# The dense value phase of a PEER layer: larger gate runs, a staged first group, other places for the row sums and the normalisation

## Chip, cores and metric

One core of a Trainium2 chip runs the whole layer. The metric is the time of one execution in microseconds (us); the median of the runs of a kernel is compared.

## The reference, cut to what matters

The layer has a mixer, a cross-attention and a PEER sublayer, 1024 tokens of width 1024, all in float32. Only the end of the PEER sublayer is touched by the change:

```python
def peer_ffn(h, w_pq, sub_keys, expert_u, expert_v):
    ...
    def block(args):
        x_blk, idx_blk, g_blk = args
        u = expert_u[idx_blk]
        a = g_blk * jax.nn.gelu(jnp.einsum('tkd,td->tk', u, x_blk), approximate=False)
        return jnp.einsum('tk,tkd->td', a, expert_v[idx_blk])
...
        ff = peer_ffn(h, w_pq[l], sub_keys[l], expert_u[l], expert_v[l])
        h = layer_norm(DN_ALPHA * h + ff, ln3_g[l], ln3_b[l])
```

There are 16384 experts, and every token picks 128 of them.

## The kernel before

`expert_stages` treats the two halves of the tokens in two ways at once. Rows 0 to 511 (four row tiles of 128 tokens, held in `xg`) are done by gathers: for each token its 128 rows of `expert_u` and of `expert_v` come in by indirect DMA. Rows 512 to 1023 are done densely: all 16384 activations are computed (`act_d`), a gate array `gate_d` holds each token's weight for each expert or zero, and the last stage, called the v phase here, multiplies activations by gates and runs one large matrix product with `expert_v`.

**Dense side.** The v phase walks over 128 expert tiles e of 128 experts, in 32 groups q of four (`GE`). For an expert tile the SP queue loads the activations (`a_raw`, 256 KB) and the rows of `expert_v` (`v_raw`, 512 KB) into two buffers each, and the gates of two expert tiles at a time (`load_gates`, 512 KB). DVE multiplies activations by gates (`multiply`, L1950), ACT rounds values and activations to their high parts (L1926, L1928), and DVE forms the low parts (`low_parts`, L1955 and L1957). PE then does, for each of four token tiles t, 24 matmuls of the group into `ps` (L106 to L108), and DVE adds the result to the accumulator `acc` (`add`, L1964). DVE's step for expert tile 4q+x contains the add of token tile x of group q-1, so DVE's step goes at the pace of PE's tiles. PE starts a group once the low parts of all its four expert tiles are there.

**Gathered side.** It shares the time of the v phase. GpSimd (POOL) issues gathers of 128 rows (512 KB each) in one fixed order, `gathers`, into a ring of 8 slots; gather n waits until gather n-8 has been used. A u gather is used by one `dot` on DVE (L1409), four v gathers by one `values` set on PE (16 narrow matmuls, L1425). `share` spreads both over the steps. Of the work left to the v phase, 96 dots belong to the first 16 groups, 6 in a group, and 64 sets are spread over all 32 groups, two in a group, behind its token tiles t=1 and t=3. Half of the sets belong to row tile 2, the other half, which need the last dots, to row tile 3.

**End.** Behind the last group, `add_residual(dve, 3)` closes the gathered rows, the residual rows of the dense half are loaded and added (L1994), and all eight row tiles are normalised: statistics and gain on DVE (`RowNorm`, L183 to L211), root and scaling on ACT, bias on POOL (L217), store by SP.

## Time and profile before

| | |
|---|---|
| median of 3 runs | 3789.56 us (3776.56 to 3790.67) |
| profiled execution: own time | 3780.85 us |
| profiled execution: span, mean granted clock | 3778.9 us, 0.912 |
| busy: PE, DVE, POOL, ACT | 83%, 56%, 38%, 32% |
| v phase in the span | from 2725.3 us to the end, 1053.6 us |

The span is from the first to the last instruction; the own time holds some 2 us more. Busy shares are averages over stages with different limits, so the v phase is read by itself, in stretches that begin where PE starts a group. Group q below is PE's group q.

### The profile page before, as it was taken

What the parts mean: (1) busy time and instruction counts of PE and PEld (TensorE: products, weight loads), DVE (VectorE), ACT (ScalarE), POOL (GpSimd) and SP (SyncE); (2) the same over time, 40 slices, a digit from 0 to 9 for tenths busy, and PEclk for the clock granted to TensorE, in tenths of its full rate; (3) what the DMA queues carried; (4) which work ended last, traced back from release to release, by engine and by line L of the source; (5) the groups of instructions that cost most, each with busy time, mean ns of one, the idle gap of its engine ahead of it and who ended that gap; (6) DMA issues with size and microseconds to landing.
All of it is one profiled execution on the core that took longest, in us unless ns stands there. A gap on an engine that the chain in (4) does not pass through costs nothing. (4 is left out here: it accounts for less than half of the span.)

```text
span 3778.9 us, 42789 instructions
## 1 busy us (share of the span) xinstructions
PE 3131.4 (83%) x16184; PEld 2426.7 (64%) x16184; DVE 2127.0 (56%) x4487; ACT 1201.8 (32%) x1931; POOL 1446.9 (38%) x1116
## 2 busy tenths in 40 slices
PE   4995978888799899999999985565378787899994
PEld 3874766777688788887777763444255565566663
DVE  4134764115422568988777765455365665555556
ACT  3113541314211244443333325666421211222221
POOL 2101011401200055557776774565445444422222
PEclk9996799899899899999999997777688998999997
DMA  4333022323222379989999996888899999988883
GB/s 151 108 98 114 1 79 87 122 75 101 94 68 67 128 298 353 335 338 397 410 410 408 411 406 242 319 296 320 302 328 343 329 341 328 330 310 308 309 311 143
DMA packets 368046, 937.45 MB, mean 248 GB/s; under 512 B 31441, under 2 KB 130265, under 8 KB 366817
## 3 DMA queue, kind: packets, MB, share of 16 engines
q0 software_dynamic: 147456, 536.94, 37.9%
q1 hardware_dynamic: 220384, 397.77, 29.9%
q8 instruction: 130, 2.13, 0.2%
q14 instruction: 76, 0.61, 0.0%
HBM read 827.60 MB, written 106.98 MB: 247 GB/s over the span
## 5 line engine op out<-in xcount | busy, mean ns | idle before, releaser
L1400 POOL DMA_INDIRECT ex_ring<-in_expert_v,ex_idxT_sb x455 | 504.4, 1109 | 604.0 <-PE ex_ps_v L1425 452.6
L1400 POOL DMA_INDIRECT ex_ring<-in_expert_u,ex_idx_sb x345 | 456.0, 1322 | 430.9 <-DVE ex_hg L1409 241.8
L1409 DVE CUSTOM_DVE_ANT_0 ex_ring<-ex_ring,ex_xg 128x1024 f32<-128x1024 f32 x345 | 413.1, 1219 | 254.7 <-DMA ex_ring<-in_expert_u,ex_idx_sb 253.8
L106 PE MATMUL eo_ps<-eo_v_hi_sb,aT_late_hi 128*128 128x512 f32 x1024 | 409.5, 400 | 41.4 <-DVE aT_late_lo L1957 41.4
L1425 PE MATMUL ex_ps_v<-ex_ring,ex_w_sb 128*32 128x512 f32 x1820 | 284.2, 716 | 170.7 <-DMA ex_ring<-in_expert_v,ex_idxT_sb 167.7
L106 PE MATMUL ex_ps_h<-aT_late_hi,ex_uT_hi_sb 128*128 128x512 f32 x1024 | 413.0, 403 | 1.9 <-ACT ex_uT_lo_sb L1541 1.1
L107 PE MATMUL eo_ps<-eo_v_lo_sb,aT_late_hi 128*128 128x512 f32 x1024 | 402.1, 393 | 0.0
L108 PE MATMUL ex_ps_h<-aT_late_hi,ex_uT_lo_sb 128*128 128x512 f32 x1024 | 401.8, 392 | 0.0
L107 PE MATMUL ex_ps_h<-aT_late_lo,ex_uT_hi_sb 128*128 128x512 f32 x1024 | 400.3, 391 | 0.0
L108 PE MATMUL eo_ps<-eo_v_hi_sb,aT_late_lo 128*128 128x512 f32 x1024 | 400.0, 391 | 0.0
L1964 DVE TENSOR_TENSOR eo_acc<-eo_acc,eo_ps 128x1024 f32<-128x1024 f32 x124 | 151.4, 1221 | 417.5 <-PE eo_ps L108 417.5
L1926 ACT ACTIVATE eo_v_hi_sb<-eo_v_raw 128x1024 fp32r<-128x1024 f32 x128 | 135.8, 1061 | 574.1 <-DMA eo_v_raw<-in_expert_v 574.1
L106 PEld LDWEIGHTS eo_ps<-eo_v_hi_sb,aT_late_hi 128*128 128x128 f32 x1024 | 193.7, 189 | 145.4 <-DVE aT_late_lo L1957 55.3
L1854 PE MATMUL ex_ps_x<-ex_hw,ex_hot 128*128 128x128 f32 x1024 | 172.8, 338 | 115.2 <-ACT ex_gate L1810 109.6
L1400 POOL DMA_INDIRECT ex_ring_more<-in_expert_u,ex_idx_sb x167 | 213.9, 1281 | 137.7 <-DVE ex_hg L1409 75.1
L1854 PEld LDWEIGHTS ex_ps_x<-ex_hw,ex_hot 128*128 128x128 f32 x1024 | 159.4, 245 | 152.7 <-issue 146.8
L1541 ACT ACTIVATE ex_uT_lo_sb<-ex_ps_t 128x1024 fp32r<-128x1024 f32 x128 | 131.7, 1029 | 379.8 <-PE ex_ps_t L1719 379.8
L1425 PEld LDWEIGHTS ex_ps_v<-ex_ring,ex_w_sb 128*32 128x32 f32 x1820 | 59.3, 124 | 296.7 <-issue 296.1
L106 PEld LDWEIGHTS ex_ps_h<-aT_late_hi,ex_uT_hi_sb 128*128 128x128 f32 x1024 | 193.0, 188 | 77.8 <-issue 30.0
L1409 DVE CUSTOM_DVE_ANT_0 ex_ring_more<-ex_ring_more,ex_xg 128x1024 f32<-128x1024 f32 x167 | 199.4, 1221 | 53.1 <-DMA ex_ring_more<-in_expert_u,ex_idx_sb 50.6
L108 PEld LDWEIGHTS eo_ps<-eo_v_hi_sb,aT_late_lo 128*128 128x128 f32 x1024 | 193.7, 189 | 41.8
L108 PEld LDWEIGHTS ex_ps_h<-aT_late_hi,ex_uT_lo_sb 128*128 128x128 f32 x1024 | 193.2, 189 | 42.6
(322 smaller groups left out, 6535.1 us busy)
## 6 DMA issues: line engine op xcount, KB each, us to landing
ex_u_raw<-in_expert_u SPq DMA_DIRECT2D x128, 512.0 KB, 8.2
eo_v_raw<-in_expert_v SPq DMA_DIRECT2D x128, 512.0 KB, 5.5
act_d<-ex_act SPq DMA_DIRECT2D x128, 256.0 KB, 6.0
gate_d<-ex_gate SPq DMA_DIRECT2D x8, 4096.0 KB, 15.9
eo_g_raw<-gate_d SPq DMA_DIRECT2D x64, 512.0 KB, 6.5
eo_a_raw<-act_d SPq DMA_DIRECT2D x128, 256.0 KB, 4.4
h_d<-n_row SPq DMA_DIRECT2D x24, 512.0 KB, 2.6
pin_raw<-in_w_in SPq DMA_DIRECT2D x20, 512.0 KB, 3.9
```

Source lines behind the costliest of these rows:

```text
L106: pe.matmul(ps, l_hi, r_hi, start=first, stop=False)
L107: pe.matmul(ps, l_hi, r_lo, start=False, stop=False)
L108: return pe.matmul(ps, l_lo, r_hi, start=False, stop=last)
L1400: pool.indirect_dma_start(rows(n), None, table, bass.IndirectOffsetOnAxis(at, 0)).then_inc(ring_in[slot[n]], 16)
L1409: dve.tensor_tensor_reduce(out=u, in0=u, in1=xg[:, j, :], scale=1.0, scalar=0.0, op0=ALU.mult, op1=ALU.add, accum_out=hg[:, j, k:k + 1]).t ...
L1425: last = pe.matmul(ps_v[32 * q:32 * q + 32, col], spreads[:, q, 31 * i + 31:31 * i + 63], rows(at[q])[:, col], start=i == 0, stop=i == 31)
L1541: act.activation(uT_lo[:, e % 2, :, :], ps_t[e % 2][:].rearrange("p (k t) -> p k t", t=P), ACT.Copy).then_inc(uT_lo_done, 1)
L1854: last = pe.matmul(ps_x[b % 2][:, x * P:(x + 1) * P], hot1[:, s, 4 * y + x, :], hw[:, s, 4 * y + x, :], start=True, stop=True)
L1926: act.activation(v_hi[:, b, x, :], v_raw(e), ACT.Copy).then_inc(v_hi_done, 1)
L1964: dve.tensor_tensor(acc[:, t, :], acc[:, t, :], ps[t % 2][:], ALU.add).then_inc(added[t % 2], 1)
```

## The change

Seven edits, all in the v phase and in the lists that feed it.

1. `load_gates` loads the gates of four expert tiles (1 MB, in two DMAs), so that each run in memory is 1 KB where it was 512 B. The second buffer for them is the part of `xg` that held row tiles 0 and 1.
2. These two row tiles, finished before, are written to `kept` (the dead DRAM buffer `h0_d`) at the start of the phase and come back into ring slots 0 and 1 at expert tile 114.
3. The four expert tiles of group 0 are loaded without waiting for each other, values into `acc`, activations into `v_sb`.
4. The residual rows of the dense half are loaded into `acc` during group 0's matmuls, and the first `add` scales and adds them; the four L1994 instructions at the end go.
5. The 96 dots are spread over the first 60 steps in place of 64. No set of values stands in groups 0, 16 and 28 to 31; 32 sets stand in groups 1 to 15 and 32 in groups 17 to 27.
6. Row tiles 0 to 3 are normalised inside groups 29 and 30 of DVE's and ACT's programs (`LN_TILES`); the order of a step is multiply, add, low parts, then the pieces of the normalisation.
7. Only row tiles 4 to 7 are normalised behind the last group, each as soon as its last add is done.

```diff
+            LAST_VALS, LN_TILES = 112, GROUPS - 3
+
+            def dots_b(e):
+                return share(DOTS_B, ETILES // 2 - 4, e) if e < ETILES // 2 - 4 else 0
+
+            def vals_b(e):
+                half = ETILES // 2
+                if GE <= e < half:
+                    return share(P // 4, half - GE, e - GE)
+                if half + GE <= e < LAST_VALS:
+                    return share(P // 4, LAST_VALS - half - GE, e - half - GE)
+                return 0
...
                     def a_raw(e):
-                        return a_sb[:, e % 2, :]
+                        return v_sb[:, e // 2, e % 2 * DN:(e % 2 + 1) * DN] if e < GE else a_sb[:, e % 2, :]
 
                     def v_raw(e):
-                        return v_sb[:, e % 2, :]
+                        return acc[:, e, :] if e < GE else v_sb[:, e % 2, :]
+
+                    def g_raw(r):
+                        flat = g_sb[:] if r % 2 == 0 else xg[:, 0:2, :].rearrange("p j d -> p (j d)")
+                        return flat.rearrange("p (n e t) -> p n e t", e=GE, t=GBLK)
...
                             def load_gates(r):
                                 if r >= 2:
-                                    sp.wait_ge(prod, 2 * (r - 1))
-                                sp.dma_start(g_raw[:, r % 2, :, :, :], gate_d[:, :, 2 * r:2 * r + 2, :].rearrange("n p e t -> p n e t")).then_inc(g_in[r % 2], 16)
...
+                                    sp.wait_ge(prod, GE * (r - 1))
+                                for h in range(2):
+                                    n = slice(h * NBLK // 2, (h + 1) * NBLK // 2)
+                                    sp.dma_start(g_raw(r)[:, n, :, :], gate_d[n, :, GE * r:GE * (r + 1), :].rearrange("n p e t -> p n e t")).then_inc(g_in[r % 2], 16)
+
+                            for e in range(GE):
+                                sp.dma_start(v_raw(e), v_rows[e, :, :]).then_inc(first_in[e], 16)
+                                sp.dma_start(a_raw(e), act_d[e, :, :]).then_inc(first_in[e], 16)
+                                if e == 0:
+                                    load_gates(0)
+                            for j in range(2):
+                                sp.wait_ge(sum_g, j + 1)
+                                sp.dma_start(kept[j * P:(j + 1) * P, :], xg[:, j, :]).then_inc(kept_out[j], 16)
...
+                                if e == GE:
+                                    for j in range(2):
+                                        sp.wait_ge(kept_out[j], 16)
+                                    load_gates(1)
+                                if e < 2 * GE:
+                                    t = e - GE
+                                    sp.wait_ge(v_lo_done, t + 1)
+                                    sp.dma_start(acc[:, t, :], resid[(GT + t) * P:(GT + t + 1) * P, :]).then_inc(row_in[t], 16)
+                                if e % GE == 2 and e // GE + 1 < GROUPS:
+                                    load_gates(e // GE + 1)
...
                                 if q == 0:
-                                    dve.tensor_copy(acc[:, t, :], ps[t % 2][:]).then_inc(added[t % 2], 1)
+                                    dve.wait_ge(row_in[t], 16)
+                                    dve.scalar_tensor_tensor(acc[:, t, :], acc[:, t, :], ALPHA, ps[t % 2][:], ALU.mult, ALU.add).then_inc(added[t % 2], 1)
...
+                                    if LN_TILES <= q < LN_TILES + GT // 2:
+                                        j = 2 * (q - LN_TILES) + x // 2
+                                        if x % 2 == 0:
...
+                                            ln.statistics(dve, j, whole_row(j))
+                                        else:
+                                            ln.scale(dve, j)
+                                        if x % 2 == 0 and j >= 1:
+                                            ln.times_gain(dve, j - 1, whole_row(j - 1))
...
-                                    for _ in range(share(VALS_B // 4, ETILES, q * GE + t)):
+                                    for _ in range(vals_b(q * GE + t)):
                                         values(pe, done)
                                         done += 4
```

Three places show how the instructions stand. The first is SP's queue at the start of the v phase, before the change; `act_d` are the activations and `gate_d` the gates.

```order
L1887 DMA eo_g_raw<-gate_d 128x8x128 x2
L1894 DMA eo_a_raw<-act_d 128x512
L1897 DMA eo_v_raw<-in_expert_v 128x1024
L1894 DMA eo_a_raw<-act_d 128x512
L1897 DMA eo_v_raw<-in_expert_v 128x1024
```

And the same place in the changed kernel:

```order
L1919 DMA eo_acc<-in_expert_v 128x1024
L1920 DMA eo_v_raw<-act_d 128x512
L1916 DMA eo_g_raw<-gate_d 128x4x256 x2
L1919 DMA eo_acc<-in_expert_v 128x1024
L1920 DMA eo_v_raw<-act_d 128x512
```

Two more such pairs follow, then two writes of kept rows (`h_d<-ex_xg`), and the regular loads begin. The queue of group 0 also takes in the gates of group 1 and four residual rows.

The second place is POOL's list of gathers at the start of the v phase, before:

```order
L1400 DMA ex_ring<-in_expert_u,ex_idx_sb 128x1024
L1400 DMA ex_ring<-in_expert_v,ex_idxT_sb 128x1024 x4
L1400 DMA ex_ring<-in_expert_u,ex_idx_sb 128x1024 x3
L1400 DMA ex_ring<-in_expert_v,ex_idxT_sb 128x1024 x4
L1400 DMA ex_ring<-in_expert_u,ex_idx_sb 128x1024 x3
```

And after:

```order
L1415 DMA ex_ring<-in_expert_u,ex_idx_sb 128x1024 x8
L1415 DMA ex_ring<-in_expert_v,ex_idxT_sb 128x1024 x4
L1415 DMA ex_ring<-in_expert_u,ex_idx_sb 128x1024 x3
L1415 DMA ex_ring<-in_expert_v,ex_idxT_sb 128x1024 x4
L1415 DMA ex_ring<-in_expert_u,ex_idx_sb 128x1024 x3
L1415 DMA ex_ring<-in_expert_v,ex_idxT_sb 128x1024 x4
L1415 DMA ex_ring<-in_expert_u,ex_idx_sb 128x1024 x3
L1415 DMA ex_ring<-in_expert_v,ex_idxT_sb 128x1024 x4
L1415 DMA ex_ring<-in_expert_u,ex_idx_sb 128x1024 x4
```

Seven more u gathers stand ahead of the first four v gathers, and further on the pieces of three u are now and then four, or one.

The third place is DVE in group 29, expert tiles 118 and 119. Before, a step there was these four rows over and over:

```order
L1950 TENSOR_TENSOR eo_a_raw<-eo_a_raw,eo_g_raw 128x512
L1964 TENSOR_TENSOR eo_acc<-eo_acc,eo_ps 128x1024
L1955 TENSOR_TENSOR eo_v_lo_sb<-eo_v_raw,eo_v_hi_sb 128x1024
L1957 TENSOR_TENSOR aT_late_lo<-eo_a_raw,aT_late_hi 128x512
L1950 TENSOR_TENSOR eo_a_raw<-eo_a_raw,eo_g_raw 128x512
```

After, the statistics of row tile 1 and the gain of row tile 0 (both in the ring) stand between two steps:

```order
L1996 TENSOR_TENSOR eo_a_raw<-eo_a_raw,ex_xg 128x512
L2011 TENSOR_TENSOR eo_acc<-eo_acc,eo_ps 128x1024
L2001 TENSOR_TENSOR eo_v_lo_sb<-eo_v_raw,eo_v_hi_sb 128x1024
L2003 TENSOR_TENSOR aT_late_lo<-eo_a_raw,aT_late_hi 128x512
L183 BN_STATS eo_ln_stats<-ex_ring 128x6 x2
L184 BN_AGGR eo_ln_mv<-eo_ln_stats 128x2
L185 TENSOR_SCALAR eo_ln_var_sb<-eo_ln_mv 128x1
L211 TENSOR_TENSOR ex_ring<-ex_ring 128x1024
L1996 TENSOR_TENSOR eo_a_raw<-eo_a_raw,ex_xg 128x512
L2011 TENSOR_TENSOR eo_acc<-eo_acc,eo_ps 128x1024
L2001 TENSOR_TENSOR eo_v_lo_sb<-eo_v_raw,eo_v_hi_sb 128x1024
L2003 TENSOR_TENSOR aT_late_lo<-eo_a_raw,aT_late_hi 128x512
```

## Rows read from the trace of the kernel before

**Rows 1.** Stretches of the v phase: start, group 0, 1 to 14, 15, 16 to 31, end.

```profile
core 0: us, PE busy (x) PEld busy (x) DVE busy (x) ACT busy (x) POOL busy (x), PEclk, DMA share, GB/s
2725.30:2749.40 24.10, 0.45 (x1) 0.18 (x1) 15.73 (x23) 6.53 (x8) 4.89 (x4) 0.50 0.82 285
2749.40:2786.60 37.20, 30.60 (x129) 21.12 (x129) 23.98 (x33) 8.35 (x10) 15.10 (x12) 0.82 0.86 299
2786.60:3268.10 481.50, 390.26 (x1793) 267.83 (x1794) 295.83 (x393) 94.12 (x113) 227.25 (x196) 0.90 0.95 336
3268.10:3295.20 27.10, 25.90 (x129) 18.58 (x130) 13.74 (x16) 4.97 (x6) 8.63 (x9) 1.00 0.90 325
3295.20:3728.30 433.10, 415.15 (x2037) 298.94 (x2041) 218.46 (x246) 101.38 (x121) 118.80 (x124) 1.00 0.83 295
3728.30:3778.90 50.60, 1.80 (x16) 0.29 (x12) 41.65 (x62) 11.54 (x16) 18.75 (x8) 0.57 0.33 125
```

**Rows 2.** Timeline of PE in group 8: its two sets of values.

```profile
3036.46 1.92 PE L1425 MATMUL ex_ps_v<-ex_ring,ex_w_sb 128*32 128x512 f32 x16 [0.17 <-DMA ex_ring<-in_expert_v,ex_idxT_sb]
3055.02 3.64 PE L1425 MATMUL ex_ps_v<-ex_ring,ex_w_sb 128*32 128x512 f32 x16 [5.53 <-DMA ex_ring<-in_expert_v,ex_idxT_sb]
```

**Rows 3.** Timeline of DVE and POOL ahead of the second set.

```profile
3039.21 1.22 DVE L1409 CUSTOM_DVE_ANT_0 ex_ring<-ex_ring,ex_xg 128x1024 f32<-128x1024 f32 x1
3040.71 1.68 POOL L1400 DMA_INDIRECT ex_ring<-in_expert_u,ex_idx_sb  x1 [4.29 <-DVE ex_hg L1409]
3046.42 1.43 POOL L1400 DMA_INDIRECT ex_ring<-in_expert_v,ex_idxT_sb  x1 [0.30 <-issue]
```

**Rows 4.** The gather line, groups 1 to 14: ns min/median/max; who waits; landing.

```profile
L1400 POOL DMA_INDIRECT ex_ring<-in_expert_v,ex_idxT_sb x115: 932/938/1892, 2786.9 to 3264.2; - x115
L1400 POOL DMA_INDIRECT ex_ring<-in_expert_u,ex_idx_sb x81: 933/1142/1683, 2790.6 to 3249.2; - x81
...
  PE ex_ps_v L1425: 91.2, 15
...
DMA to landing us min/median/max: 5.0/6.7/10.9
```

**Rows 5.** DMA in groups 1 to 14: queues, then issues with KB and median landing.

```profile
q0 software_dynamic: 28234, 102.81, 58.2%
q1 hardware_dynamic: 45292, 58.84, 36.2%
...
eo_a_raw<-act_d SPq DMA_DIRECT2D x56, 256.0 KB, 4.7
eo_g_raw<-gate_d SPq DMA_DIRECT2D x28, 512.0 KB, 9.5
```

**Rows 6.** Stretches with much and with little in 512 B runs; columns as Rows 1.

```profile
2000.00:2100.00 100.00, 95.33 (x495) 72.33 (x494) 81.94 (x245) 35.12 (x40) 68.01 (x56) 0.98 1.03 409
2728.00:2731.00 3.00, 0.00 (x0) 0.00 (x0) 0.00 (x0) 0.00 (x0) 0.00 (x0) 0.50 1.15 327
```

**Rows 7.** Timeline of PE in the second half: sets behind t=3, t=1, t=3.

```profile
3428.31 1.92 PE L1425 MATMUL ex_ps_v<-ex_ring,ex_w_sb 128*32 128x512 f32 x16
3442.57 1.92 PE L1425 MATMUL ex_ps_v<-ex_ring,ex_w_sb 128*32 128x512 f32 x16
3455.57 1.92 PE L1425 MATMUL ex_ps_v<-ex_ring,ex_w_sb 128*32 128x512 f32 x16
```

**Rows 8.** Timeline of PE from group 30 to group 31.

```profile
3700.91 1.92 PE L1425 MATMUL ex_ps_v<-ex_ring,ex_w_sb 128*32 128x512 f32 x16
...
3704.03 0.50 PE L106 MATMUL eo_ps<-eo_v_hi_sb,aT_late_hi 128*128 128x512 f32 x1 [1.20 <-DVE aT_late_lo L1957]
```

**Rows 9.** Timeline of DVE and POOL in the end stretch.

```profile
3730.16 1.22 DVE L1458 SCALAR_TENSOR_TENSOR ex_xg<-ex_xg,ex_ps_v 128x1024 f32<-128x1024 f32 x1 [0.66 <-PE ex_ps_v L1425]
3733.75 1.41 DVE L183 BATCH_NORM_STATS2 eo_ln_stats<-ex_xg 128x6 f32<-128x512 f32 x2
3735.52 1.22 DVE L211 TENSOR_TENSOR ex_xg<-ex_xg,ex_w_sb 128x1024 f32<-128x1024 f32 x1
3744.07 3.27 DVE L1994 SCALAR_TENSOR_TENSOR eo_acc<-eo_v_raw,eo_acc 128x1024 f32<-128x1024 f32 x1
...
3743.91 2.34 POOL L217 TENSOR_TENSOR ex_xg<-ex_xg,ex_w_sb 128x1024 f32<-128x1024 f32 x1 [1.16 <-DVE ex_xg L211]
...
3773.51 2.34 POOL L217 TENSOR_TENSOR eo_acc<-eo_acc,ex_w_sb 128x1024 f32<-128x1024 f32 x1 [1.16 <-DVE eo_acc L211]
```

More of the change, by code:

```diff
@@ L1253, in _, with expert_stages @@
                         scores(HP - 1)
-        def expert_stages(gain, bias, resid, dest):
+        def expert_stages(gain, bias, resid, kept, dest):
             GT = 4
@@ L1317, in expert_stages @@
             END_G = len(gathers)
-            for n in range(GE * (GROUPS + 1)):
-                for _ in range(share(DOTS_B, ETILES // 2, n) if n < ETILES // 2 else 0):
+            for e in range(ETILES + GE):
+                for _ in range(dots_b(e)):
                     gathers.append(("u", nu))
                     nu += 1
-                for _ in range(4 * share(VALS_B // 4, ETILES, n - GE) if n >= GE else 0):
+                for _ in range(4 * vals_b(e - GE)):
                     gathers.append(("v", nv))
@@ L1362, in expert_stages @@
             row_in = [sem(f"eo_row_in{i}") for i in range(DT)]
-            sum_done, stored = sem("eo_sum"), sem("eo_stored")
+            first_in = [sem(f"eo_first_in{i}") for i in range(GE)]
+            kept_out, kept_in = [[sem(f"eo_kept_{w}{i}") for i in range(2)] for w in ("out", "in")]
+            stored = sem("eo_stored")
             with ExitStack() as whole:
@@ L1862, in expert_stages @@
                     sb, pb = local(stage)
[L1863 removed]
+                    ln = RowNorm("eo_ln", sb, gain, bias, rows=(ring[:, 2, :], ring[:, 3, :]))
                     acc = sb("eo_acc", [P, DT, D])
[L1865 removed]
+                    a_sb, v_sb, g_sb = sb("eo_a_raw", [P, 2, DN]), sb("eo_v_raw", [P, 2, D]), sb("eo_g_raw", [P, 2 * D])
                     a_hi, a_lo = [w[:].rearrange("p (b x) t -> p b x t", b=2) for w in (late_hi, late_lo)]
@@ L1907, in _ @@
+                                if e < 2 * GE:
[4 more added lines that the diff above has]
+                                    load_gates(e // GE + 1)
+                                if e == LAST_VALS + 2:
                                     sp.wait_ge(val_done, GT * P // 4)
+                                    for j in range(2):
+                                        sp.dma_start(whole_row(j), kept[j * P:(j + 1) * P, :]).then_inc(kept_in[j], 16)
@@ L1968, in _ @@
                             spread_weights(dve, 2)
-                            for q in range(GROUPS + 1):
+                            for q in range(GROUPS):
                                 if q == VAL_TILE:
```

90 lines of the change are left out of this document (43 added, 47 removed).

## Prediction

> **What bounds the kernel now.** I read first the stretches of the v phase, because nothing before 2725 us changes [rows 1]. There are three regimes.
>
> In groups 1 to 14 a group takes 481.5 / 14 = 34.4 us, while in group 15, which has the same matmuls and the same two sets but no dots beside it, it takes 27.1 us. The 7 us between them are PE waiting. The timeline of PE says for what: the set behind t=1 starts at once, the one behind t=3 waits 5.5 us for its gathers and then takes 3.64 us where 1.92 is usual [rows 2]; in the 14 groups such waits are 91.2 us, 15 times [rows 4]. Following one back: the tile t=1 ends about 3036.3, DVE does its add and low parts and then the dot at 3039.21, which frees the slot for the u gather at 3040.71, four v gathers must follow it in POOL's order, the last is issued at 3046.42, and the set starts at 3055.02 [rows 2, 3]. So this stretch is set by the ring. In numbers: 115 + 81 = 196 gathers, 14 a group, 2.46 us a gather, so that with 8 slots a slot turns round in 19.7 us, of which the landing (median) is only 6.7 [rows 4]. The rest is order and waiting for PE's and DVE's steps. The DMA engines are nearly always busy too, 0.95 [rows 1], but at 336 GB/s, where the same core moves 409 at a share of 1.03 earlier on [rows 6]. So they are loaded, and not quite the limit.
>
> In groups 16 to 31 the 433.1 us are PE's own [rows 1]. A set and two tiles take 13.00 us and, over a group boundary, 14.26 [rows 7]. At the boundary PE ends its last tile at about 3700.9, DVE has still to add, and to make the low parts of the last expert tile, and PE starts again at 3704.03: 3.1 us, of which a set behind t=3 hides 1.9 [rows 8]. So a tile is about 5.5 us, a set not at t=3 costs 2.0, a boundary 3.1 whether a set lies in it or not: 16 x 22.0 + 15 x 3.1 + 16 x 2.0 = 430.5, against 433.1 measured.
>
> In the end stretch, 50.6 us, DVE is busy for 41.7 and PE for 1.8 [rows 1].
>
> **The change, part by part.**
>
> *Start.* Now 24.1 us, in which DVE works 15.7 [rows 1]; the staged loads remove only what DVE waits between the four expert tiles, since four dots and the same splitting stay. The first multiply still has 1.75 MB ahead of it or with it. Gain 0 to 4, I take 2.
>
> *Group 0* has no sets any more. From 37.2 go the two sets, 1.9 and 3.5, and a wait of some 6.5; its boundary is bare again, +3.1. The new instruction that waits is the first add of a token tile, for its residual row; behind it in DVE stand the low parts of group 1. The residual row of t=3 is queued behind 1 MB of gates and the loads of expert tiles 6 and 7, and 1 MB of kept rows has gone out before. I give this 1 us; at worst it is 8. New 29.3, so 8 gained.
>
> *Groups 1 to 13.* Dots go from 6 to 6.4 a group, v gathers from 8 to 8.53: 14.93 gathers where there were 14. If the ring keeps its 2.46 us a gather, a group takes 36.7, and 13 groups 477.1 in place of 447.2: 30 lost. The other bound is that the transfers set the pace. The two queues take 58.2% and 36.2% of 34.4 us [rows 5], which is 20.0 for 14 gathers (1.43 each) and 12.5 for the loads. The added 0.93 gathers are +1.3. The gates: in the stretch that is mostly 512 B runs the core moves 327 GB/s, and 409 in one with few of them [rows 6], so a group's 1.05 MB takes 3.2 us and, if 1 KB runs brought it all the way, 2.6. By the share (1.15 against 1.03) it is a little more. I take 0.8 saved, between 0 and 1.1. Then a group is (32.5 + 1.3 - 0.8) / 32.5 x 34.4 = 34.9, and 13 groups lose 7. I take the ring's end, because of the 19.7 us only 6.7 are landing, so lighter transfers shorten little of it.
>
> The Trainium skill's page "DMA: Bandwidth & Descriptors", section Specifications, gives 512 B as the smallest transfer that reaches line rate; by it 1 KB runs would save nothing, and the transfers' end would be 35.8 a group. The trace disagrees in part: 327 against 409 GB/s. By either, the ring's 36.7 stays.
>
> *Groups 14 and 15.* The dots are over, and each is PE's own: four tiles, boundary, and two sets not at t=3, 22.0 + 3.1 + 4.0 = 29.1. Together 58.2 where 34.4 + 27.1 = 61.5 stood: 3 gained.
>
> First half in all: -2 - 8 + 30 - 3 = +17.
>
> *Groups 16 to 31.* The same 32 sets now stand in 11 groups, and in only 8 of these one stands at t=3. The boundaries behind groups 16 to 19 and 28 to 30 are bare. By the formula, 352 + 46.5 + 24 x 2.0 = 446.5, and with the 2.6 that the formula lacks 449.1: +16. The sets of three tiles in a row ask for their last gathers 12.7 us after a slot comes free, and four issues (about 1.24 apart) with a landing of 6.7 need 10.4 to 12; I add 4 for late ones.
>
> The normalisation in groups 29 and 30 costs DVE time in steps that are now only 5.5 us. A step is 3.5; statistics add 1.8 and the gain 1.1 [rows 9]. Then POOL adds the bias, 2.34, and while it runs, a DVE instruction with two operands in SBUF waits: L1994 takes 3.27 beside POOL's L217, and the same operation with one operand in PSUM takes 1.22 [rows 9]. The multiply and the low parts have two such operands. Walking through the steps, the low parts of the last expert tile are 2.0 late in group 29 and 2.8 in group 30. PE waits both: +5. Second half: 16 + 4 + 5 = +25.
>
> *End.* PE's last tile, then DVE: add 1.1, statistics 1.8, gain of the tile before 1.2, scale 0.3, then ACT 1.3, gain about 2 with POOL in the way, POOL 2.34, and from its end to the end of the span 3.05 [rows 1, 9]: 13.2 with the small gaps. It was 50.6 behind the same tile. Gain 37.4.
>
> *Hidden.* The return of the kept rows and the gain and bias loads come when DMA has no gathers left. The first adds cost as much as the copies they replace.
>
> **Sum.** +17 + 25 - 37.4 = +4.6. Against the profiled execution's own 3780.85 that is 3785.5. The median of the runs is 8.7 above that execution and the lowest 4.3 below; the mean of all four is 3784.4. I forecast 3786, that is, no change. Half a per cent, 19 us, is about what can be told from nothing.
>
> **The rivals.**
>
> *Transfers set the first half (faster).* For it speak the DMA share of 0.95 [rows 1], and that the gates' landing is 9.5 us among gathers, against 4.7 for the activations [rows 5]: fewer, larger packets could let all else land sooner. Against it the 336 GB/s. Groups 1 to 13 then lose 7 in place of 30: 3785.5 - 23 = 3762.5. If also the late sets of the second half vanish, 3758.
>
> *The loads fall behind in groups 17 to 27 (slower).* A group there has 11.6 gathers, where groups 16 to 31 have 8: 11.6 x 1.43 + 12.5 - 0.8 = 28.3 us of transfers in 29.5 us of PE, a share of 0.96, as in the first half. Activations of expert tile 4q+3 are issued one step after the 1 MB of gates and are needed about two steps after them, some 15 us, with up to 4 more until the add waits for PE. The gates' 512 KB took 9.5 among gathers; 1 MB in as many packets as 512 KB had, but longer ones, takes 10 to 14, and the activations 5 more: 15 to 19. It decides from 19 on. If it is 2 us late in 11 groups, +22: 3807; 3 us, 3818.
>
> The same page, section Queues, rings and completion order, says each DMA engine takes a packet from each queue in turn. By that rule the gates' small packets wait for a gather's large one each time, as the 9.5 us suggest, and halving their number should shorten this wait. No row shows 1 KB runs.
>
> *The end gives nothing back.* It would need that DVE or POOL were not what holds the end stretch; DVE's 41.7 of 50.6 exclude it.
>
> **Chances.** Forecast, within 0.5%: 0.45, own range 3770 to 3803. Transfers set the pace: 0.30. Loads fall behind: 0.25. From these faster 0.30, same 0.45, slower 0.25. The range reaches to the first rival's 3758 and a little below, and over the second's milder form: 3756 to 3811, about 0.2 left out.
>
> **What the profile after would show.** The end stretch behind PE's last eo_ps matmul is 11 to 16 us. Groups 1 to 13 take 36 to 37.5 us with gather waits of 5 to 9 us before a set in most groups; if they take under 35, the transfers' theory holds. Groups 28 to 30 have no L1425 line (now L1440), and a wait of 3 to 6 us on the low parts ahead of each group. In groups 17 to 27 DVE should not wait for DMA at the multiply; if it does, for tens of us in total, the second rival holds. I am wrong by more than the range if group 0 stalls on the kept rows, or if the granted clock falls in groups that now wait longer.

## The result, and the profile after

The changed kernel takes 3840.58 us (median of 4 runs, 3834.19 to 3843.32), the kernel before beside it 3785.32 (4 runs). The ratio is 1.0146, 95% interval 1.0130 to 1.0163: slower by 55 us, where 3786 was forecast.

The stretches of the v phase after the change, cut where PE starts group 0, 1, 14 and 16 and behind its last matmul (us; busy time and count of PE, PEld, DVE, ACT, POOL; clock; DMA share; GB/s). They answer to [rows 1], where the second cut behind group 0 is at group 15 in place of 14:

```profile
2725.30:2745.00 19.70, 0.00 (x0) 0.00 (x0) 14.06 (x21) 7.47 (x9) 5.41 (x4) 0.50 1.02 381
2745.00:2776.50 31.50, 24.27 (x97) 19.57 (x97) 22.41 (x31) 5.60 (x7) 8.78 (x7) 0.88 0.96 358
2776.50:3266.30 489.80, 378.33 (x1681) 257.15 (x1681) 279.56 (x375) 87.27 (x105) 221.50 (x191) 0.89 0.88 316
3266.30:3326.70 60.40, 56.15 (x273) 38.84 (x274) 31.21 (x38) 13.63 (x17) 19.36 (x19) 0.97 0.80 287
3326.70:3824.90 498.20, 434.49 (x2049) 310.25 (x2049) 244.12 (x295) 107.07 (x134) 133.95 (x130) 0.95 0.73 264
3824.90:3838.10 13.20, 0.00 (x0) 0.00 (x0) 6.25 (x9) 1.83 (x3) 5.92 (x3) 0.63 0.29 119
```

The end stretch fell from 50.6 to 13.2 us, as worked out. The forecast for the first half was +17; start, group 0, groups 1 to 13 and groups 14 and 15 came to -4.4, -5.6, +42.7 and -1.2, in all +31.5 (before, groups 1 to 13 took 447.1 and groups 14 and 15 61.7). The second half was to cost +25 and cost +65 (498.2 against 433.1). In both the DMA engines are less busy than before (0.88 and 0.73, before 0.95 and 0.83), and the clock of PE is lower (0.95 against 1.00 in the second half). So on average the DMA engines had less to do, not more; PE waited in more places, and slowed down behind the waits. In groups 1 to 13 its waits for gathers are about the same before (first row) and after (second row); new are the waits for the low parts at the start of a group (third row, with the 7.2 ahead of group 1), of which there were none:

```profile
PE ex_ps_v L1425 <- DMA ex_ring<-in_expert_v,ex_idxT_sb: 84.4, 14, 7.7
PE ex_ps_v L1440 <- DMA ex_ring<-in_expert_v,ex_idxT_sb: 89.1, 15, 7.9
PE eo_ps L106 <- DVE aT_late_lo L2003: 26.4, 9, 7.2
```

The table of waits for groups 15 to 31 (who, for what: us, times, longest) names one that was not there before, DVE's for activations, and one that has grown: PE waits 66.7 us for low parts where it had 18.0. The longest wait of either kind belongs to group 28 and is explained under group 27.

```profile
PE eo_ps L106 <- DVE aT_late_lo L2003: 66.7, 16, 14.5
DVE eo_a_raw L1996 <- DMA eo_a_raw<-act_d: 45.3, 10, 16.6
```

**Groups 18 to 23** take 203.9 us in all, 34.0 each. Their three sets stand behind t=0, 1 and 2 in groups 18 and 19, behind t=0, 1 and 3 in 20 to 22, behind t=0, 2 and 3 in 23, and the timeline of group 18 (SP's issues, then DVE and ACT, then PE) shows what happens:

```profile
3392.30 1.63 SPq L1916 DMA_DIRECT2D eo_g_raw<-gate_d  x2
3399.02 0.33 SPq L1929 DMA_DIRECT2D eo_a_raw<-act_d  x1
...
3405.87 0.69 DVE L2003 TENSOR_TENSOR aT_late_lo<-eo_a_raw,aT_late_hi 128x512 fp32r<-128x512 f32 x1
3411.73 0.69 DVE L1996 TENSOR_TENSOR eo_a_raw<-eo_a_raw,ex_xg 128x512 f32<-128x512 f32 x1 [5.17 <-DMA eo_a_raw<-act_d]
...
3414.28 1.06 ACT L1967 ACTIVATE eo_v_hi_sb<-eo_v_raw 128x1024 fp32r<-128x1024 f32 x1 [14.01 <-DMA eo_v_raw<-in_expert_v]
...
3415.37 1.22 DVE L2001 TENSOR_TENSOR eo_v_lo_sb<-eo_v_raw,eo_v_hi_sb 128x1024 fp32r<-128x1024 f32 x1 [1.82 <-ACT eo_v_hi_sb L1967]
...
3417.25 0.79 PE L106 MATMUL eo_ps<-eo_v_hi_sb,aT_late_hi 128*128 128x512 f32 x1 [6.06 <-DVE aT_late_lo L2003]
```

The gates of the next group, 1 MB, are issued at 3392.30, the activations of the fourth expert tile at 3399.02, its values right behind them; POOL issues twelve gathers between 3390.60 and 3409.55. The multiply is ready at 3406.6 and starts at 3411.73, 19.4 us after the gates' issue and 12.7 after its own load's. The values land later still, at 3414.3, and DVE waits another 1.82 us until ACT has split them. PE then waits 6.06 at the boundary, where a bare boundary is 3.05. So it is the values, queued behind the late activations, that end last here; in groups 20 to 22 DVE waits 0.50 to 0.55 us for them behind the late multiply. Later on, in groups 24 to 26, with three sets a group as well, but spread to t=0, 2 and 3 or 1, 2 and 3, PE has no such wait. The first row below is groups 18 to 22, the second 24 to 26 (columns as above); the late loads fall where the DMA share is 0.82, not where it is 0.97.

```profile
3381.20:3553.20 172.00, 148.15 (x720) 100.17 (x720) 71.59 (x81) 33.88 (x41) 58.98 (x60) 0.95 0.82 304
3585.10:3673.20 88.10, 84.51 (x433) 57.13 (x433) 42.92 (x49) 19.41 (x24) 34.75 (x37) 1.00 0.97 355
```

**Group 27** took 42.6 us. PE's timeline has its longest wait at the start of group 28, and the waits of SP's own queue show why: SP stood for 17.4 us, until the last set of values, ahead of the loads of the two kept rows (L1948).

```profile
3715.82 0.79 PE L106 MATMUL eo_ps<-eo_v_hi_sb,aT_late_hi 128*128 128x512 f32 x1 [14.48 <-DVE aT_late_lo L2003]
```

```profile
SPq L1948 <- PE ex_ps_v L1440: 17.4, 1, 17.4
```

**Groups 1 to 13** are not even: with sets behind t=1 and 3 (groups 1 to 3, 9 to 11) they average 35.5, in groups 5 to 7, 12 and 13, where they stand behind t=0 and 2, 39.9. (Group 4 has t=1 and 2, group 8 three sets.)

### The profile page after: what moved, and what is told of

It is laid out like the page before. It is cut to its first block and busy times, and to the rows that moved or that the text cites. A ratio compares the mean times of both kernels' runs of the same rounds, so it can differ in the third digit from the quotient of the medians.

```text
span 3838.1 us, 42758 instructions
## 1 busy us (share of the span) xinstructions
PE 3156.1 (82%) x16184; PEld 2442.2 (64%) x16184; DVE 2116.9 (55%) x4483; ACT 1198.1 (31%) x1931; POOL 1446.2 (38%) x1116
## 5 line engine op out<-in xcount | busy, mean ns | idle before, releaser
L106 PE MATMUL eo_ps<-eo_v_hi_sb,aT_late_hi 128*128 128x512 f32 x1024 | 424.0, 414 | 117.8 <-DVE aT_late_lo L2003 117.8
L107 PE MATMUL eo_ps<-eo_v_lo_sb,aT_late_hi 128*128 128x512 f32 x1024 | 413.0, 403 | 0.0
L108 PE MATMUL eo_ps<-eo_v_hi_sb,aT_late_lo 128*128 128x512 f32 x1024 | 410.0, 400 | 0.0
L2011 DVE TENSOR_TENSOR eo_acc<-eo_acc,eo_ps 128x1024 f32<-128x1024 f32 x124 | 151.3, 1220 | 438.4 <-PE eo_ps L108 438.3
L106 PEld LDWEIGHTS ex_ps_h<-aT_late_hi,ex_uT_hi_sb 128*128 128x128 f32 x1024 | 192.8, 188 | 77.5 <-issue 29.8
L107 PEld LDWEIGHTS eo_ps<-eo_v_lo_sb,aT_late_hi 128*128 128x128 f32 x1024 | 201.1, 196 | 40.2
```

Of the source, the lines that this page charges most:

```text
L106: pe.matmul(ps, l_hi, r_hi, start=first, stop=False)
L107: pe.matmul(ps, l_hi, r_lo, start=False, stop=False)
L108: return pe.matmul(ps, l_lo, r_hi, start=False, stop=last)
L2011: dve.tensor_tensor(acc[:, t, :], acc[:, t, :], ps[t % 2][:], ALU.add).then_inc(added[t % 2], 1)
```

## The experiments

The work ahead of the v phase is the same in all kernels, but takes from 2742.8 to 2776.4 us by the profiled executions. The medians come from several chips, on which the kernel before takes 3779.7 to 3804.6, so rows are compared by their ratios and not by their medians. Beside the ratio of whole times (each against the kernel before on the same chip) this table gives the profiled stretch from PE's first matmul of the v phase to the end of the span, and parts of it; these are of one execution each.

| kernel | median us | ratio (95%) | v stretch | groups 1-13 | 17-27 |
|---|---|---|---|---|---|
| before | 3785.3 | | 1029.5 | 447.1 | 299.8 |
| after | 3840.6 | 1.0146 (1.0130-1.0163) | 1093.1 | 489.8 | 364.0 |
| late wait moved | 3837.0 | 1.0101 (1.0074-1.0129) | 1074.3 | 482.6 | 353.7 |
| + gate halves | 3806.9 | 1.0038 (1.0012-1.0064) | 1044.0 | 469.6 | 335.3 |
| + sets at t=1,2,3 | 3813.6 | 1.0045 (1.0027-1.0064) | 1043.3 | 484.0 | 320.8 |
| + odd sets, first half | 3796.6 | 0.9992 (0.9973-1.0011) | 1032.9 | 445.0 | 351.4 |
| all four | 3732.6 | 0.9873 (0.9857-0.9890) | 997.9 | 439.5 | 322.4 |
| + one row tile a group | 3724.0 | 0.9855 (0.9836-0.9874) | 975.7 | 423.2 | 323.5 |
| + double steps even | 3723.1 | 0.9788 (0.9766-0.9809) | 944.5 | 384.3 | 320.8 |
| same, sets from group 0 | 3708.2 | 0.9745 (0.9723-0.9768) | 943.6 | 388.1 | 322.4 |

"+" in the fourth to sixth row is added to the moved wait alone; "all four" are the moved wait and these three, and below it each is added to the row above.

### The late wait

```diff
-                                if e == LAST_VALS + 2:
+                                if e == LAST_VALS + 5:
```

> The changed kernel with one move: SP's wait for the last set of values, and the four loads behind it, stand behind expert tile 117 in place of 114. Theory A (SP's wait holds the loads of expert tile 115, which PE needs for group 28): group 27 falls from 42.6 us to 29 to 30, the wait of 14.5 us ahead of group 28 to 3, and the run is about 13 us faster than the changed kernel, 3827. Rival (group 28 waits because 2 MB of returning rows and gains stand ahead of its loads in the queue, wherever the wait is): the wait moves to group 28 or 29 and the time changes by under 4 us.

Group 27 went from 42.64 to 29.39 us, and PE starts group 28 after an ordinary wait:

```profile
3716.34 0.50 PE L106 MATMUL eo_ps<-eo_v_hi_sb,aT_late_hi 128*128 128x512 f32 x1 [1.20 <-DVE aT_late_lo L2003]
```

So the wait for the last set at expert tile 114 cost 13 us: SP reached it while PE was still in group 27, and the loads of tile 115 were queued behind it. The rival, that the returning rows delay group 28 wherever the wait stands, is out. The whole time agrees by its ratio (1.0101 against 1.0146, 17 us), not by its median, since the kernel before takes 3796.8 on this chip. All edits below to the changed kernel are made on top of this one.

### Gates in two steps; other places in the second half

```diff
-                                if e % GE == 2 and e // GE + 1 < GROUPS:
-                                    load_gates(e // GE + 1)
+                                if e % GE in (1, 2) and e // GE + 1 < GROUPS:
+                                    load_gates(e // GE + 1, (e % GE - 1,))
```

> As the kernel with the late wait, and the two halves of a group's 1 MB of gates are issued behind expert tiles 4q+1 and 4q+2 in place of both behind 4q+2. Theory B (in groups 18 to 23 the activations of expert tile 4q+3 land late because 1 MB of gates stands ahead of them): DVE's waits for the activations, 45 us after group 15, fall under 20, groups 18 to 23 go from 204 us towards 180, 15 to 25 us faster than the late wait alone. Rival (the sets behind t=0, 1, 2 call their twelve gathers into the same 20 us, whatever the gates do): under 8 us faster.

```diff
                 if half + GE <= e < LAST_VALS:
-                    return share(P // 4, LAST_VALS - half - GE, e - half - GE)
+                    return 1 if e % GE and e != 69 else 0
```

> As the kernel with the late wait, but the 32 sets of groups 17 to 27 stand behind t=1, 2 and 3 (group 17 has two), as already in groups 26 and 27. Every boundary of these groups is then covered. Theory B' (clumps of gathers at t=0, 1, 2 over the gates make the loads late, and bare boundaries add 3 us): groups 17 to 27 take 29.4 us each, 323 us in place of 350, 20 to 28 us faster. Rival (2.9 sets a group are too many transfers wherever they stand, share 0.96): under 8 us faster.

The first leaves every gather where it was and only issues half of the gates one step earlier: groups 18 to 23 go from 206.9 to 187.2 us (180 was expected; the boundaries behind groups 18 and 19 stay bare). The second leaves the loads and moves the sets away from t=0: groups 18 to 27 take 29.35 each, which is 22.0 + 3.1 + 2 x 2.0 and the 0.2 that the formula lacked. DVE's wait for activations over the second half, in the first and in the second kernel:

```profile
DVE eo_a_raw L1996 <- DMA eo_a_raw<-act_d: 5.2, 6, 1.7
```

```profile
DVE eo_a_raw L1996 <- DMA eo_a_raw<-act_d: 3.8, 4, 1.5
```

It was 27.3 us in the kernel with the late wait alone. Either edit takes nearly all of it away, so it took both, 1 MB of gates in one step and the three sets close together.

### What a bare boundary costs

The kernel before, with its 64 sets behind t=0 and t=2 in place of t=1 and t=3:

```diff
-                for _ in range(4 * share(VALS_B // 4, ETILES, n - GE) if n >= GE else 0):
+                for _ in range(4 * (1 - n % 2) if n >= GE else 0):
...
-                                    for _ in range(share(VALS_B // 4, ETILES, q * GE + t)):
+                                    for _ in range(1 - t % 2):
```

> The kernel before with one change: its 64 sets stand behind t=0 and t=2 of each group in place of t=1 and t=3. Same work, same number of gathers in a group. Theory C (what costs is the boundary that no set, and no wait for one, covers): groups 1 to 14 go from 34.4 us to 38 to 40, groups 16 to 30 from 27.26 to 29.1 to 29.4, so 50 to 75 plus 30 us slower than before: 3865 to 3890. Rival (the place of a set does not matter where gathers set the pace): groups 1 to 14 stay at 34 to 35, only 30 us slower.

It takes 3846.21 us, ratio 1.0152 (1.0122 to 1.0182). In groups 16 to 30 nothing but this place differs: 30.7 us in place of 27.26, so 3.45 for a set that leaves t=3, where the working had 2.0. Of this, 1.85 are idle time (3.05 at a boundary in place of 1.20); the other 1.6 are PE's slower work. Behind each 3.05 us of idle time it starts at the lower clock, and the mean granted clock over 200 us, six and a half such groups, is 0.95 (first row), in the kernel before 1.00 (second).

```profile
3400.00:3600.00 200.00, 181.69 (x845) 129.75 (x845) 92.78 (x104) 43.00 (x52) 50.48 (x52) 0.95 0.76 269
```

```profile
3400.00:3600.00 200.00, 190.43 (x939) 136.06 (x939) 103.19 (x116) 48.14 (x58) 57.90 (x60) 1.00 0.87 308
```

Cut finer, at the boundary at 3427.77: the granted clock is 0.50 (1.2 GHz) for the 3.3 us that begin with PE's start, and 1.00 (2.4 GHz) from there to the next boundary.

```profile
3427.40:3430.70 3.30, 2.93 (x7) 2.38 (x8) 0.92 (x2) 0.63 (x1) 0.00 (x0) 0.50 1.02 382
3430.80:3458.00 27.20, 24.60 (x122) 17.23 (x121) 13.24 (x15) 6.02 (x7) 7.73 (x8) 1.00 0.74 261
```

So the first matmuls behind such a wait are 0.43 us apart from the second on, and 0.23 once the clock is full.

```profile
3427.77 0.80 PE L106 MATMUL eo_ps<-eo_v_hi_sb,aT_late_hi 128*128 128x512 f32 x1 [3.05 <-DVE aT_late_lo L1957]
3428.36 0.63 PE L107 MATMUL eo_ps<-eo_v_lo_sb,aT_late_hi 128*128 128x512 f32 x1
3428.78 0.63 PE L108 MATMUL eo_ps<-eo_v_hi_sb,aT_late_lo 128*128 128x512 f32 x1
```

### The first half: places, rhythm, or loads

```diff
                 if GE <= e < half:
-                    return share(P // 4, half - GE, e - GE)
+                    return e % 2 + (e in (58, 62))
```

> As the kernel with the late wait, but the 32 sets of groups 1 to 15 stand behind t=1 and t=3, with the two extra ones behind t=2 of groups 14 and 15. The number of gathers in a group is as in the changed kernel. Theory C (a group boundary with no set behind t=3 costs its 3.05 us on top of the wait for gathers, and the groups with sets at t=0 and 2 take 39.9 us where those with t=1 and 3 take 35.5): groups 1 to 13 go from 490 us to about 462, 25 to 30 us faster. Rival (the ring sets the pace by its gathers alone, or transfers do): under 8 us faster.

Groups 1 to 13 went from 482.6 to 445.0 us, 34.2 a group. The expectation takes the number of gathers as unchanged, which is not quite so: with the extra sets in groups 14 and 15, two sets a group and 6.4 dots make 14.4, and POOL issues 185 gathers in groups 1 to 13 where it issued 191. At the ring's 2.46 us each, 14.4 gathers ask for 35.4, so this run alone does not decide against the ring; the price of a gather in it, 2.41 us, is near the old one. And in the kernel above, sets behind t=0 and 2 had cost the first half almost nothing (451.2 against 447.1). Two more kernels, profiled in one execution each, split this up; the first is the changed kernel with the old dots (96 over 64 steps), the second the old kernel with sets behind t=0 and 2 and the new dots (96 over 60 steps).

```diff
-                return share(DOTS_B, ETILES // 2 - 4, e) if e < ETILES // 2 - 4 else 0
+                return share(DOTS_B, ETILES // 2, e) if e < ETILES // 2 else 0
```

> The changed kernel with the late wait and with the dots over 64 steps, 3 in 2 steps, as before the change; its sets stay where the change put them. If it is the dots' new rhythm together with sets at t=0 and 2 that costs, groups 5 to 8, 12 and 13 fall from 38 to 42 us to 34 to 36, 20 to 30 us less in the first half. If the loads do it (1 MB of gates at once), they stay at 38 to 42.

```diff
-                                        for _ in range(share(DOTS_B, ETILES // 2, q * GE + x)):
+                                        for _ in range(share(DOTS_B, 60, q * GE + x) if q < 15 else 0):
```

> The kernel before with its sets at t=0 and 2 and the dots over 60 steps, 8 in 5. If the rhythm and the place together suffice, its groups 1 to 13 rise from 34.7 us to 37 to 41. If they need the new loads too, they stay at 34 to 36.

They took 3830.77 and 3909.78 us, groups 1 to 13 471.5 and 500.7. The first fell short of what was expected of the old rhythm: 11 us less in groups 1 to 13, not 20 to 30, and group 14 gave 8 of them back (37.3 us in place of 29.3). The second has none of the new loads and is slow all the same, so these are not needed for it. Its groups go in a pattern of five: groups 4 and 9 take 35, the others 37 to 41. With 1.6 dots a step, the steps with two dots wander, and a set's four v gathers start later when its own step has two. The rows are DVE's dots, POOL's first v gather and PE's set, in the second of these kernels (group 3):

```profile
2893.65 1.22 DVE L1409 CUSTOM_DVE_ANT_0 ex_ring<-ex_ring,ex_xg 128x1024 f32<-128x1024 f32 x1
2894.80 1.22 DVE L1409 CUSTOM_DVE_ANT_0 ex_ring<-ex_ring,ex_xg 128x1024 f32<-128x1024 f32 x1
...
2897.13 0.94 POOL L1400 DMA_INDIRECT ex_ring<-in_expert_v,ex_idxT_sb  x1 [0.30 <-issue]
...
2910.53 3.64 PE L1425 MATMUL ex_ps_v<-ex_ring,ex_w_sb 128*32 128x512 f32 x16 [6.79 <-DMA ex_ring<-in_expert_v,ex_idxT_sb]
```

and in the kernel of the section before, with the old rhythm, where the step has one dot (group 3 too):

```profile
2869.54 1.22 DVE L1409 CUSTOM_DVE_ANT_0 ex_ring<-ex_ring,ex_xg 128x1024 f32<-128x1024 f32 x1
...
2871.04 1.15 POOL L1400 DMA_INDIRECT ex_ring<-in_expert_v,ex_idxT_sb  x1 [7.46 <-DVE ex_hg L1409]
...
2883.92 3.00 PE L1425 MATMUL ex_ps_v<-ex_ring,ex_w_sb 128*32 128x512 f32 x16 [4.29 <-DMA ex_ring<-in_expert_v,ex_idxT_sb]
```

From the first dot to the first v gather it is 3.48 us with two dots and 1.50 with one, since a u gather stands ahead in POOL's order and takes the slot that the first dot frees. To test it, the old kernel with two dots in even steps and one in odd ones (before: one and two), the list of gathers changed with them, with sets at either place:

```diff
-                                        for _ in range(share(DOTS_B, ETILES // 2, q * GE + x)):
+                                        for _ in range(2 - x % 2 if q < GROUPS // 2 else 0):
```

> The kernel before with its sets behind t=0 and t=2 and the dots still 1.5 a step in the first 64 steps, but two in the even steps and one in the odd ones (before: one and two). If what matters is where a step with two dots stands ahead of the gathers of the second set, each of groups 1 to 13 is like the late ones of the kernel with 1.6 dots a step: 37 to 41 us, and PE's first matmul of a group follows a bare boundary of 3.05. If what matters is only that 1.6 dots are more than 1.5, a group stays at 34 to 35 as with sets behind t=0 and 2 and the old rhythm.

> The same dots, two in the even steps and one in the odd ones, but the sets at the old places, t=1 and t=3. If the set at t=3 takes up what the dots' places cost, a group stays at 33 to 35 us. If the dots' places cost by themselves, it is 37 or more as in the other kernel.

One execution each: 3922.75 and 3727.51 us, against 3786.02 for the kernel before beside them. The first came as expected. The second did not: the two answers on record were 33 to 35 us a group, or 37 and more, and it took 29.8. With the sets at their old places the list of gathers is the same as before, only DVE does every third dot one step sooner. So the ring rule falls here: the same 182 gathers take 2.46 us each in one order of dots and 2.12 in the other. All of it together, in us a group (mean of groups 1 to 13, one execution a cell; the left cell of the second row is the changed kernel with its new loads, all others are the old one):

| dots in a set's own step | sets behind t=1, 3 | behind t=0, 2 |
|---|---|---|
| one | 29.8 | 34.7 |
| one or two, wandering | 34.2 | 38.5 |
| two | 34.4 (before) | 38.9 |

Each row and each column has its price: 4.2 to 4.6 us for the double step in a set's own step, 4.3 to 4.9 for the bare boundary. PE's waits in groups 1 to 13 say the same: from the kernel before to the fast corner (the cell of 29.8) its waits for gathers fall from 84.4 to 42.6 us, and from the fast corner to the cell at its right 13 boundary waits of 3.05 come in while the waits for gathers stay (41.2). The rest comes with the granted clock, which is 0.90 before, 0.99 in the fast corner and 0.93 at its right. So the even sets had cost the first half nothing only because they left the double steps as well, and the two cancelled. That the wandering rhythm costs nearly as much as the constant double step is measured and not explained. In the fast corner the DMA engines are busy throughout (groups 0 to 14 of that kernel, all but the last 1.6 us):

```profile
2768.60:3213.10 444.50, 396.44 (x1908) 285.56 (x1912) 312.48 (x419) 98.73 (x120) 224.89 (x206) 0.98 1.02 383
```

That transfers are the limit there is read from this share and not shown by a run.

### 1 KB runs

```diff
...
-                                    n = slice(h * NBLK // 2, (h + 1) * NBLK // 2)
-                                    sp.dma_start(g_raw(r)[:, n, :, :], gate_d[n, :, GE * r:GE * (r + 1), :].rearrange("n p e t -> p n e t")).then_inc(g_in[r % 2], 16)
+                                    sp.dma_start(g_raw(r)[:, :, 2 * h:2 * h + 2, :], gate_d[:, :, GE * r + 2 * h:GE * r + 2 * h + 2, :].rearrange("n p e t -> p n e t")).then_inc(g_in[r % 2][h], 16)
...
```

The gates in 512 B runs again, two expert tiles at a time and at their old places; first with the odd sets of the first half, then in the version with one row tile a group.

> The kernel with the first-half sets at t=1 and 3, with gates again in 512 B runs, two expert tiles a load, at the old places in SP's queue; all else as there. Theory of the ring (a gather costs its turn whatever the loads do): groups 1 to 13 stay at 445 us. Theory of the transfers (1 KB runs and fewer packets are what let 14.9 gathers a group take 34.2 us where 14 took 34.4): 13 x 2 = 20 to 35 us more. In groups 18 to 23 the smaller loads should also remove some of the lateness of the activations, 197 us towards 185.

> The kernel with one row tile normalised a group, with gates in 512 B runs and two expert tiles a load at the old places in SP's queue. Theory of the transfers (1 KB runs save DMA time that PE sees): 10 us or more slower. Theory that the size of the runs does not reach the end time, only how the gates are spread over the steps: within 6 us of that kernel, on either side.

They took 3761.99 us, ratio 0.9958 (0.9942 to 0.9974), and 3740.12, ratio 0.9876 (0.9856 to 0.9896). Groups 1 to 13 took 434.2 and 438.4 us; with 1 KB runs the same sets gave 445.0, 439.5 and 423.2. The last two of these are the same program there, so 16 us is what one execution differs from another, and the runs' length is worth nothing beyond it. The old places also spread the gates over the steps, which is why groups 18 to 23 fall from 203.0 to 190.8 us in the first of the two. The second is 8 us slower by its ratio than its neighbour with 1 KB runs (0.9855), with intervals that overlap: neither of its two expectations, within 6 us or 10 and more. By the Trainium skill, page "DMA: Bandwidth & Descriptors", section Specifications, 512 B is already enough for line rate: these runs agree.

### The normalisation

```diff
-            LAST_VALS, LN_TILES = 112, GROUPS - 3
+            LAST_VALS, LN_TILES = 112, GROUPS + 1
...
+                            for j in range(GT):
...
+                                ln.statistics(dve, j, whole_row(j))
+                                if j >= 1:
+                                    ln.times_gain(dve, j - 1, whole_row(j - 1))
+                                ln.scale(dve, j)
```

> The kernel with the late wait, and all eight row tiles normalised behind the last group (the residual is still added first). Theory D: groups 28 to 30 lose their lag, 84 us become 75 to 76, and the end stretch grows from 13 to 33 to 36 us: in sum about 12 us slower than the late wait alone. It also prices what normalising inside the groups gives: 21 us for 9. Rival (no lag by the normalisation): groups 28 to 30 stay at 84.

With all eight row tiles normalised behind the last group (and the late wait moved) it takes 3844.17 us, 1.0176 (1.0159 to 1.0193). Groups 28 to 30 take 78.6 us in place of 84.0, so the normalisation in them cost 5.4 as the prediction had it (+5; the expectation above has 8 to 9), and the stretch behind the last matmul is 37 us in place of 13.

```diff
-                                    if LN_TILES <= q < LN_TILES + GT // 2:
-                                        j = 2 * (q - LN_TILES) + x // 2
-                                        if x % 2 == 0:
+                                    if q >= LN_TILES:
+                                        j = q - LN_TILES
+                                        if x == 0:
...
-                                        else:
+                                        elif x == 1:
                                             ln.scale(dve, j)
-                                        if x % 2 == 0 and j >= 1:
-                                            ln.times_gain(dve, j - 1, whole_row(j - 1))
+                                        elif x == 2:
+                                            ln.times_gain(dve, j, whole_row(j))
...
```

> As the kernel with all three, but one row tile is normalised in each of groups 29, 30 and 31, its gain two steps behind its statistics, and the fourth behind the last low parts. Theory D (two row tiles a group make DVE late, and PE waits 5.4 and 6.0 us for the low parts ahead of groups 29 and 30 where 3.05 is bare): groups 28 to 30 go from 27.5, 30.3 and 27.6 us to 25 to 26 each, 8 to 10 us faster than all three, and the end stretch stays within 2 us of 13. Rival (the gain and bias collide with DVE's steps in any place): under 3 us.

This is the version with all four edits above, and one row tile normalised in each of groups 29, 30 and 31, in DVE's steps x=0 (statistics), 1 (scale) and 2 (gain), the fourth behind the last low parts. Groups 28 to 30 take 77.6 us in place of 86.2; the waits ahead of groups 29 and 30 are 3.27 and 3.26, near the bare 3.05, where they had been 5.39 and 5.98:

```profile
3629.40 0.50 PE L106 MATMUL eo_ps<-eo_v_hi_sb,aT_late_hi 128*128 128x512 f32 x1 [3.27 <-DVE aT_late_lo L2006]
3654.72 0.58 PE L106 MATMUL eo_ps<-eo_v_hi_sb,aT_late_hi 128*128 128x512 f32 x1 [3.26 <-DVE aT_late_lo L2006]
```

### Put together

> The changed kernel with the late wait, the gate halves apart, the sets of groups 1 to 15 at t=1 and 3, and those of groups 17 to 27 at t=1, 2 and 3. If the causes found (SP's wait 13 us, bare boundaries in the first half 37, clumps and bare boundaries in the second 32, of which the gate halves alone had given 20) lie apart, groups 1 to 13 take about 440 us, 17 to 27 take 321, and from PE's first dense matmul to the end it is 990 to 1000 us, against 1029.5 before: 30 us faster than the kernel before, ratio 0.991 to 0.993. Rival (the waits only move): 1015 or more.

> The kernel with one row tile normalised a group, but dots over 64 steps and sets at t=1 and 3 from group 0 on, just as before the change: 14 gathers a group, 1 KB gates in halves. If the gathers of a group set its pace, groups 1 to 14 take 33 to 34 us each, about 470 in all, where that kernel takes 423 for 1 to 13 and 30.2 for 14, so 15 us slower or more, since group 14 is again among the slow ones and group 0 has its sets back. If gates and staging had helped the first half by themselves, groups 1 to 14 would fall under 32 each.

```diff
             def dots_b(e):
-                return share(DOTS_B, ETILES // 2 - 4, e) if e < ETILES // 2 - 4 else 0
+                return 2 - e % 2 if e < ETILES // 2 else 0
```

> The fastest version so far (odd sets in groups 1 to 15, sets at t=1, 2, 3 in groups 17 to 27, half gates, one row tile normalised a group; 3724 us), with the dots two in even and one in odd steps up to expert tile 63. If the place of the double steps is what the first half waits for, groups 1 to 13 go from 423 us to about 13 x 29.7 = 386 and the time to about 3685. If the effect belongs to the gather list of the old kernel, it stays at 3715 to 3730.

> The same, but with the sets behind t=1 and t=3 from group 0 on as in the kernel before (its form with the old rhythm took 3756 us, groups 0 to 15 550 us). With the new place of the double steps groups 0 to 15 should take some 472 us as in the kernel before with the same dots, and the time be about 3680. Without the effect it stays at 3756.

All four edits gave 3732.64. The first half with dots and sets as in the kernel before gave 3756.13, ratio 0.9925 (0.9908 to 0.9941), groups 1 to 13 451.5: all else in the change, mended, is worth 0.75% by itself. With the double dots in even steps its groups 1 to 13 take 388.1 and the kernel 3708.22 us, ratio 0.9745 (0.9723 to 0.9768), 2.5% faster than before; 3680 had been expected, on a chip where the kernel before takes 3779.7 and not 3804.6. With no set in group 0 it is 384.3 (386 was expected) and 3723.06; its profiled v stretch is as short (944.5 against 943.6), though its group 14, with three sets and six dots, takes 39.3. Both have 1 KB runs, and the old kernel with the same dots and 512 B runs took 386.7 in groups 1 to 13: the runs' length shows nothing there either.

## Why the prediction was wrong

**The start, group 0, groups 14 and 15, the end**: right within 3 us each, and the end exactly. The rival that the end gives nothing back is out.

**Groups 1 to 13, "If the ring keeps its 2.46 us a gather": this step failed.** The size was near (+30 forecast, +42.7 measured), the reason was not, and the nearness is in part luck. The count was too high, since groups 1 to 13 hold 27 sets and not their share of 32 in 15 groups: 191 gathers, 14.7 a group, for which 2.46 us ask for 469 us or +22. And 2.46 us was no property of the ring: the same list of gathers runs at 2.46 us each or at 2.12, by the order of the dots alone (34.4 and 29.8 us a group). It was the waiting of one order of dots against sets, divided by the gathers. In the changed kernel PE's waits for gathers rose by 5 us only; 22 us came in at the boundaries (26.4 without the 7.2 ahead of group 1 and with the 3.05 ahead of group 14), and more time at the lower clock. The cost came from two things that the working passed over, though the first was in its own formula for the second half: sets behind t=0 and t=2 leave the boundary bare, and the new rhythm puts double steps where some of the sets are. Had I followed the rows of one set from dot to gather to set for each place, and not only for the old one, both were to be had [rows 2, 3].

**The rival "Transfers set the first half"** finds no support for this kernel and the one before: 1 KB runs bring nothing beyond what executions differ, the 327 GB/s that spoke for them are read from 3 us [rows 6], and the old kernel had 4.6 us a group in it that only the order of the dots cost.

**Groups 16 to 31.** The formula for PE's own time holds where nothing waits (29.35 and 25.1 us). What it had too small is the price of a bare boundary, 3.45 and not 2.0, as the clock falls behind it; the prediction names a falling clock among the ways to be wrong, and gives it no price.

**"I add 4 for late ones": this step failed too.** The 4 us were for late gathers, and in groups 17 to 27 PE waited for no gather at all. Late were the loads, which the sum had at nothing; the second rival was the right mechanism, given 0.25 only. Its threshold, 19 us from the gates' issue, was about right, and 19.4 was reached. Its cover of 4 us was right as well: in group 18 PE's last tile ends at 3411.19 and the add waits for it in any case, while the late multiply ends at 3412.42, so only 1.2 of DVE's 5.17 us reach PE. The other 1.8 of PE's 3.0 us beyond the bare boundary are the values of the same expert tile, queued behind the activations, of which the rival did not speak. Its place was wrong: six groups with clumped sets, not eleven, and clumping, not the share of 0.96. By the runs groups 17 to 27 took 34 us more than the working's 330: 13 the late wait, 18 to 20 the late loads.

**SP's wait at expert tile 114 was missed.** The working said "The return of the kept rows and the gain and bias loads come when DMA has no gathers left", and gave them no time. It did not price the wait ahead of them in SP's queue, for a set that PE had yet to do, nor the loads behind it. This is 13 us.

**The normalisation's lag** was +5 and is 5.4; with the bare boundaries and the clock behind the longer waits groups 28 to 30 took 86.9 against the 80.8 of the working.

In sum: 17 + 25 - 37.4 was forecast, 31.5 + 65 - 37.4 came.

## What to carry to other kernels

A mean time per gather, taken from a stretch in which engines wait for one another, holds those waits and says nothing of another order; follow one item through the ring for each order that is compared. A wait put into a queue delays all that is queued behind it: look at how far the waiting queue runs ahead of the engine that it waits for. Where one piece of filler work covers a fixed wait at a boundary, moving it away costs the wait and the clock behind it. And where consumers free slots in order, it paid here to do the double step one step ahead of the one that needs them.

## What was not expected of the hardware

Idle times of PE of only 3.05 us at each boundary put its granted clock at 0.50 for some 3.3 us behind each, 0.95 in the mean over 200 us, and added 1.6 us to a group beside the idle time itself; idle times of 1.20 us left it at 1.00. And the load of 256 KB that took 5.7 us in the median of groups 17 to 22 took 12.7 where it followed 1 MB of gates, while POOL issued twelve gathers in 19 us, at a mean DMA share of only 0.82.
